# Two FFN projections in seven half-width products instead of eight, for eight of eleven block pairs

## The reference, cut to what matters

```python
def swiglu_ffn(h, w_in, w_out):                 # fa; h = rms_norm(x, g), hidden 2816
    gate, up = jnp.split(h @ w_in, 2, axis=-1)
    return (jax.nn.silu(gate) * up) @ w_out

def swiglu(h, w_gate, w_up, w_down):            # fb and fc, same sizes
    return (jax.nn.silu(h @ w_gate) * (h @ w_up)) @ w_down
```

## Time and profile before

| | |
|---|---|
| median of 3 runs | 2423.3 us (2422.54 to 2423.92) |
| span of the profiled execution | 2420.5 us |
| time around that span, by the median | 2.8 us |
| TensorE busy | 2397.5 us |
| VectorE, ScalarE, GpSimd busy | 1263.9, 1002.5, 331.9 us |
| bytes read | 231.83 MB |

### The profile page before, as it was taken

One profiled execution on the slowest core, in us unless ns is written; L12 is line 12 of the kernel. 1 busy time (PEld: TensorE's weight loads), 2 busy tenths in 40 slices (PEclk: granted clock), 3 DMA queues, 4 the chain that ended last, 5 costly groups with the idle time before them and its releaser, 6 DMA issues.

```text
span 2420.5 us, 30412 instructions
## 1 busy us (share of the span) xinstructions
PE 2397.5 (99%) x12064; PEld 1956.4 (81%) x12064; DVE 1263.9 (52%) x1907; ACT 1002.5 (41%) x1634; POOL 331.9 (14%) x258
## 2 busy tenths in 40 slices
PE   8999999999999999999999999999999999999998
PEld 7777778777898888888888888888887888888887
DVE  5688746468765455443333544333678555333422
ACT  7766654234563344333223433222644454323321
POOL 0000000555100100111102111101032201101100
PEclk9999999999999999999999999999999999999999
DMA  6221235323665232332323332332322232333231
GB/s 203 71 70 51 86 99 183 113 68 108 200 210 209 96 105 70 105 95 88 96 97 101 99 97 90 96 100 88 111 63 63 87 113 74 101 96 105 97 100 56
DMA packets 172638, 251.65 MB, mean 104 GB/s; under 512 B 11472, under 2 KB 90576, under 8 KB 172496
## 3 DMA queue, kind: packets, MB, share of 16 engines
q1 hardware_dynamic: 171344, 248.13, 32.5%
q10 hardware_dynamic: 1152, 1.57, 0.2%
HBM read 231.83 MB, written 16.78 MB: 103 GB/s over the span
## 4 chain that ended last, share of the span: by engine, by line
PE 96%; DVE 2%; ACT 1%; issue 0%; POOL 0%; DMA 0%; DVEq 0%; SPq 0%; POOLq 0%
PE bank L1170 94%; PE bank L1299 1%; DVE wlo L2030 0%; PE bank L1322 0%; DVE T L2038 0%; PE bank L1447 0%; PE bank L1423 0%; DVE macc L2030 0%; PE bank L1265 0%; DMA raw<-in_w_in 0%; DVE xg L2034 0%; ACT whi L1541 0%; DVE ml L2038 0%; DVE bank L2336 0%; DVE W L2030 0%
## 5 line engine op out<-in xcount | busy, mean ns | idle before, releaser
L1170 PE MATMUL bank<-xh,whi 128*128 128x512 f32 x1784 | 710.1, 398 | 8.0 <-DVE wlo L2030 8.0
L1170 PE MATMUL bank<-xh,wlo 128*128 128x512 f32 x1784 | 696.6, 390 | 0.0
L1170 PE MATMUL bank<-xl,whi 128*128 128x512 f32 x1784 | 695.9, 390 | 0.0
L2030 DVE TENSOR_TENSOR wlo<-raw,whi 128x1024 fp32r<-128x1024 f32 (+2 forms) x406 | 500.2, 1234 | 337.2 <-ACT whi L1541 337.0
L1541 ACT ACTIVATE whi<-raw 128x1024 fp32r<-128x1024 f32 (+2 forms) x406 | 419.2, 1038 | 513.7 <-PE bank L1170 507.2
L1170 PEld LDWEIGHTS bank<-xh,whi 128*128 128x128 f32 x1784 | 335.7, 188 | 94.7 <-issue 20.2
L1170 PEld LDWEIGHTS bank<-xh,wlo 128*128 128x128 f32 x1784 | 335.4, 188 | 71.1
L1170 PEld LDWEIGHTS bank<-xl,whi 128*128 128x128 f32 x1784 | 336.0, 188 | 65.4
L2030 DVE TENSOR_TENSOR T<-bank,R 128x512 f32<-128x512 f32 x86 | 59.0, 687 | 344.3 <-PE bank L1170 344.3
L1170 PE MATMUL bank<-hh,whi 128*128 128x512 f32 (+1 forms) x536 | 206.9, 386 | 0.0
L1170 PE MATMUL bank<-hl,whi 128*128 128x512 f32 (+1 forms) x536 | 206.8, 386 | 0.0
(11 more groups left out here) (356 smaller groups left out, 3494.9 us busy)
## 6 DMA issues: line engine op xcount, KB each, us to landing
raw<-in_w_in SPq DMA_DIRECT2D x92, 512.0 KB, 3.6
raw<-in_w_ffn_in SPq DMA_DIRECT2D x88, 256.0 KB, 3.2
raw<-in_ffn_gate SPq DMA_DIRECT2D x88, 256.0 KB, 2.8
raw<-in_ffn_up SPq DMA_DIRECT2D x88, 256.0 KB, 3.1
raw<-in_ffn_down SPq DMA_DIRECT2D x44, 512.0 KB, 3.6
raw<-in_w_ffn_out SPq DMA_DIRECT2D x22, 512.0 KB, 3.6
raw<-in_w_xattn_kv SPq DMA_DIRECT2D x16, 512.0 KB, 4.4
raw<-in_w_kv_mem SPq DMA_DIRECT2D x16, 512.0 KB, 4.9
```

The source lines that it names most:

```text
L1170: return e.matmul(out, l, r, start=start, stop=stop, skip_group_check=skip)
L2030: return e.tensor_tensor(out, a, b, op)
```

## The change

For blocks 3 to 10 of each FFN the pair of projections is computed in seven products instead of eight (a Winograd form of the 2 x 2 block product). Tokens are cut in halves of 256, the eight row chunks in even and odd ones, the 256 gate and 256 up columns of a block in two tiles of 128 each. Then a product is (four chunks) x (128 gate and 128 up columns) x (256 tokens): 2 x 4 x 3 = 24 matmuls with 256 moving columns, all in one bank, gate in its left half and up in its right one.

- **Operands.** `operands(tag)` makes, beside blocks 0 to 2, the normalized x in quarters, three sums and differences and the high and low parts of all seven, in `xop` (four buffers of 14 x 256): `x_gain`, `op_hi` on ScalarE, `x_norm`, `x_sum`, `op_lo` on VectorE. As R is in them, these blocks need no multiplication by R.
- **Weights.** A block's weights come as two quarters of 1 MB (`load_quarter`; even and odd chunks) to four buffers. Four of the seven weight operands are sums: two on GpSimd (products 5 and 6), two on VectorE (7 and 3). All seven are split as slots are (`s_hi`, `s_lo`), three products ahead.
- **Joins.** ScalarE copies bank a to bank b after product 1 (`seed_b`) and bank b to bank f after product 7 (`seed_f`), and TensorE adds later products onto the copies; it copies two partial results to T buffers (`keep`), which VectorE adds (`c22`, `c12`). Then silu of 256 columns on ScalarE and a multiplication with the up half on VectorE (`s_mul`), four times a block, write `hid`.
- **Banks.** Odd blocks use side, even ones main, and block 1 and d0 are moved to side.
- **Hidden tensor.** `ffn_up` writes `hid`; its high and low parts (`h_hi`, `h_lo`) are made at the end of the seven-product stretch and during d0, as are fb's `x_scaled` steps.
- **Memory.** The DMA scratch is cut to 1 KB so that the buffers fit.

```diff
+        def product_order():
+            order = [(PLAIN, p) for p in (1, 5, 6, 2)]
+            for i in range(PLAIN + 1, 11):
+                order += [(i - 1, 7), (i, 1), (i - 1, 4), (i, 5)]
+                order += [(i - 1, 3), (i, 6), (i, 2)]
+            return order + [(10, 7), (10, 3), (10, 4)]
...
+        def seven(tag):
+            first = SEVEN[tag] + len(PRODUCTS)
...
+            for n, (i, p) in enumerate(PRODUCTS):
...
+                step("product", tag, n)
+                pay()
+                owed.append(lambda i=i, p=p: seven_finished(tag, i, p))
+                point()
+                prepare_sum(tag, n + 4)
+                prepare_last(tag, n + 6)
+                prepare_hi(tag, n + 3)
...
+            def product(tag, n):
...
+                w.wait_ge(*at("w lo", c))
+                if p in (1, 5):
+                    ring, name = seven_ring(i)
+                    w.wait_ge(*free(ring, name, u))
+                elif p in (2, 6):
+                    w.wait_ge(*at("seed b", tag, i))
+                elif p == 7:
+                    w.wait_ge(*at("kept", tag, i, 6))
+                elif p == 4:
+                    w.wait_ge(*at("seed f", tag, i))
+                else:
+                    w.wait_ge(*at("kept", tag, i, 5))
+                for gu in range(2):
+                    out = b[:, 256 * gu:256 * gu + 256]
+                    for k in range(4):
...
+                        a, d = h[:, gu, k, :], l[:, gu, k, :]
+                        t, tl = xopr[k][:, hi, :], xopr[k][:, lo, :]
+                        mm(out, a, t, p in (1, 5) and gu == 0 and k == 0, False, skip=True)
+                        mm(out, a, tl, False, False, skip=True)
+                        ins = mm(out, d, t, False, k == 3, skip=True)
...
+            def seed_b(tag, i):
+                ring, name = seven_ring(i)
+                u, b = seven_bank("b", tag, i)
+                w.wait_ge(*free(ring, name, u))
+                w.wait_ge(*at("product", tag, i, 1))
+                copy(b[:], seven_bank("a", tag, i)[1][:]).then_inc(*up("x_exp", ("seed b", tag, i)))
...
+            def w_sum(tag, i, p):
+                if p not in COMBINED:
+                    return
...
+                if p == 5:
+                    ins = tt(out, part_of(tag, i, 7), part_of(tag, i, 4), ALU.add)
+                else:
+                    w.wait_ge(*at("w sum", tag, i, 5))
+                    ins = tt(out, part_of(tag, i, 5), part_of(tag, i, 1), ALU.subtract)
+                ins.then_inc(*up("ffn_gate", ("w sum", tag, i, p)))
...
         def ffn(tag, out):
...
-            for i in range(11):
+            for i in range(PLAIN):
...
-                        soon(1, "h_lo", tag, 2 * i + m - 2)
-                gemm(f"{tag}{i}", evict)
-            step("mark", f"{tag}d")
+                gemm(f"{tag}{i}", evict, hook=begin_seven(tag) if i == PLAIN - 1 else None)
+            drain(built[0])
+            seven(tag)
+            for x, j in enumerate(range(4, 22)):
+                soon(max(0, 2 * x - 2), split_h, tag, j)
+            if tag == "fb":
+                for k in range(8):
+                    soon(4 + 4 * k, "x_scaled", k)
             gemm(f"{tag}d0", residual(out, 0))
```

More of the change, by code:

```diff
@@ L13 @@
 S = 512
-BASE = 17408
+SCRATCH = 1024
+BASE = SCRATCH + 1024
 EPS = 1e-6
@@ L334, in split_to @@
         def split_to(j):
-            while ready[0] < min(j, NS):
+            while ready[0] < min(j, upto[0]):
                 load_to(ready[0] + NR)
@@ new lines, in begin_seven, with hook @@
+        def begin_seven(tag):
+            def hook(n):
+                if n == 4:
+                    for i in range(PLAIN, 11):
+                        for e in range(2):
+                            step("quarter", tag, i, e)
+                if n in (11, 13, 15):
+                    prepare_hi(tag, (n - 11) // 2)
+                if n in (12, 14):
+                    prepare_sum(tag, n // 2 - 5)
+            return hook
+        def seven(tag):
+            first = SEVEN[tag] + len(PRODUCTS)
+            ready[0] = loaded[0] = first
+            upto[0] = min([x for x in SEVEN.values() if x > first] + [NS])
+            for n, (i, p) in enumerate(PRODUCTS):
+                ring = seven_ring(i)[0]
+                if p == 1:
+                    for b, letter in enumerate("aebf"):
+                        ring.new(letter, tag, i, among=(b,))
+                    for b, what in enumerate(("even", "odd", "c22", "u2")):
+                        (tmp2 if i % 2 else tmp).new(what, tag, i, among=(b,))
+                step("product", tag, n)
[5 more added lines that the diff above has]
+                prepare_hi(tag, n + 3)
+                if (i, p) == (8, 5):
+                    split_h(tag, 0)
+                if n >= PLACE[9, 3] + 3:
+                    split_h(tag, n - PLACE[9, 3] - 2)
+                if n + 3 >= len(PRODUCTS):
+                    split_to(first + n + 4 - len(PRODUCTS))
+            step("mark", f"{tag}d")
@@ L935, in ffn, with build @@
         def ffn(tag, out):
+            built = []
+            def build():
+                built.append(start(operands(tag), 3))
             if tag == "fb":
@@ L956, in ffn, with ahead @@
             else:
-                later(1, norm(tag))
+                def ahead():
+                    norm(tag)()
+                    soon(5, build)
+                later(1, ahead)
             step("mark", f"{tag}")
-            for i in range(11):
+            for i in range(PLAIN):
                 def evict(m, i=i):
@@ L1887, in ffn_gate, with h_hi @@
                 e.activation(t[:], t[:], ACT.Silu).then_inc(*up("ffn_silu", ("ffn silu", tag, j)))
-            def ffn_up(tag, j):
-                n, t = tmp("gate", tag, j)
+            def h_hi(tag, j):
+                w.wait_ge(*at("h done", tag, j))
+                if 0 < j < 5:
+                    for q in (11, 22, 21, 12):
+                        w.wait_ge(*at("s mul", tag, 9, q))
+                elif j > 4:
+                    w.wait_ge(*at("product", tag, 10, 3))
+                copy(hh[j][:], hid[j][:]).then_inc(*up("h_hi", ("h hi", tag, j)))
@@ new lines, in op_hi, with s_hi @@
+            def op_hi(tag, kp, part):
+                t, tr = xop[kp], xopr[kp]
+                if part == 0:
+                    w.wait_ge(*at("x norm", tag, kp))
+                    ins = copy(tr[:, 11:14, :], t[:, 8:11, :])
+                else:
+                    w.wait_ge(*at("x sum", tag, kp))
+                    w.wait_ge(*at("op lo", tag, kp, 0))
+                    ins = copy(tr[:, 7:11, :], t[:, 0:4, :])
+                ins.then_inc(*up("x_hi", ("op hi", tag, kp, part)))
+            def s_hi(tag, n):
+                i, p = PRODUCTS[n]
+                c = SEVEN[tag] + n
+                if p in (1, 2, 4):
+                    w.wait_ge(*at("quarter", tag, i, 0 if p == 1 else 1))
+                else:
+                    w.wait_ge(*at("w sum", tag, i, p))
+                w.wait_ge(*at("w used", c - NH))
+                copy(eight(shi[c % NH][:]), part_of(tag, i, p)).then_inc(*up("w_hi", ("w hi", c)))
```

316 lines of the change are left out of this document (286 added, 30 removed).

## The result

The changed kernel takes 2393.6 us (median of 4 runs, 2392.6 to 2396.5) where the kernel before takes 2422.9 on the same chip: ratio 0.9881, 95% interval 0.9867 to 0.9895, or 29.3 us less. The forecast was 2389.5 and 33.7 us. The profiled execution has a span of 2390.8 us, 29.7 under the one before.

The account below looks back on a forecast made before the run. TensorE, busy 99% of the span, was taken as the bound. 38.2 us saved in blocks less 4.5 at entries gives 33.7 off 2420.5, 2386.8; with 2.8 carried over, 2389.6, rounded 2389.5 us; range 2382 to 2408.

Parts of the forecast that it names:

- the largest term of the sum: TensorE in the changed blocks: 1.59 us saved a block, 38.2 us for 8 blocks x 3 FFNs.
- The rate: TensorE block by block: a plain block takes 21.67 us, a changed one 20.08 at 0.1195 us a matmul.
- Rival 3: TensorE in changed blocks: a matmul is paid by its columns alone, 60 us saved, 2363 us; chance 0.03.
- The other engines: Per changed block: ScalarE 11.4 us, VectorE 14.4 and up to 18.5 with contention, all hidden within TensorE's 20.1.
- The joins: TensorE's new waits for copies or joins at five of seven products: 0 us in steady state, 2 us spare.
- Rival 1: The joins leak in changed blocks: one wait late by 0.6 to 1.2 us, 14 to 29 us in all; chance 0.17.
- The weights: Quarter loads in the changed blocks: 4 to 7 us each, 0 us cost, but the steady chain's least cover.
- The entry: Start of each FFN's eight changed blocks: late second weight sum and bank copy, 4.5 us for three FFNs, bounds 0 and 9.
- 1.5 with what follows: Loss at each FFN's entry: 1.4 us taken for the late sum and copy, 1.5 including what comes after.
- the contention: GpSimd and VectorE slow one another in changed blocks: VectorE loses at most about 4 us a block, hidden.
- Exit: Hidden tensor's high and low parts moved to the down projection: TensorE needs nothing of it early, 0 us.

Follow-up runs that it names:

- the narrow kernel: Changed kernel with 192 of 256 moving columns in every matmul of the seven-product stretch; one run, 0.1117 us between starts, no whole time given.
- Five plain blocks: Changed kernel with five plain blocks instead of three in each FFN, six changed blocks fewer in all: 2401.36 us, 9.4 us slower than the changed kernel.
- the seven doubled low parts: Changed kernel with each low part of a weight operand computed twice on VectorE, in all seven products: 2514.75 us, 123 us slower than the changed kernel.
- a second copy: Changed kernel with each of a block's four bank copies made twice on ScalarE: 2393.53 us, 1.6 us slower than the changed kernel.
- The early second sum: Changed kernel with product 6's first-block sum issued ahead of the last two gate multiplications on GpSimd: 2388.48 us, 3.5 us faster than the changed kernel.
- the sums on VectorE: Changed kernel with all four weight sums of a block on VectorE, none on GpSimd: 2385.89 us, 6.1 us faster than the changed kernel.
- keeping the third one back: Sums on VectorE plus early second sum, with the second block's first quarter not loaded until the first block's quarters are there: 2385.64 us.
- the kernel with four copies: Changed kernel with each of a block's four bank copies made four times on ScalarE: 2411.93 us, 20 us slower than the changed kernel.

## Why the prediction was right, and where it was off

The mechanism was right: TensorE's rate sets the blocks, the other engines are hidden, and the loss is at the entries. That the largest term of the sum came out to 0.2 us was luck, two misreadings that cancel.

**The rate.** A changed block was put at 168 x 0.1195 = 20.08 us and takes 20.16, at 0.1200 a start: in the two stretches of the earlier trace rows the first few steps are shorter, and the others are 0.120. A plain block was put at 96 x 0.2257 = 21.67 and takes 21.76, by the count that was read too high. Each term is too low by 0.08 or 0.09 us, and so their difference, the saving, is 1.60 us where 1.59 was predicted: 38.4 in all against 38.2. Had only one of them been read rightly, the sum would have been off by some 2 us. Rival 3, columns alone, is out twice over, by the rate and by the narrow kernel. With it goes the Trainium skill's 262 cycles for 256 columns (TensorE: Matmul & The Clock Gate, Back-to-back issue gap) as a price for this stream: 109 ns there, which the page calls the gap of an isolated matmul, and 120 here. Five plain blocks show the saving per block by a timing of its own.

**The other engines.** ScalarE was put at 11.4 us a block and has 10.8; VectorE at 14.4 plus at most 4 and has 15.6; GpSimd at up to 5.8 when alone and has 5.6. Nothing of it is on the path, and the seven doubled low parts show where it would be.

**The joins.** "0 us in steady state, 2 us spare" is right: no wait in 21 of 24 blocks, a second copy free, and three more cost a steady block 0.09 us. Rival 1 didn't happen.

**The weights.** 0 us in the steady part, right. The cover was thinner at fb's entry than said, below.

**The entry.** This is the term that was mis-sized: 4.5 us predicted, 2.3 + 3.3 + 2.3 = 7.9 measured. The first wait comes at the place and in the size worked out. GpSimd and VectorE at fa's entry in the changed kernel, first product at 1037.35 (T):

```profile
1035.45 1.30 POOL L3141 TENSOR_TENSOR T<-T,R 128x512 f32<-128x512 f32 x1 [2.43 <-ACT T L2097]
1036.92 2.07 POOL L3141 TENSOR_TENSOR T<-T,R 128x512 f32<-128x512 f32 x1 [0.17 <-ACT T L2097]
1038.95 2.39 POOL L3141 TENSOR_TENSOR wsum<-wsum,quarter 128x1024 f32<-128x1024 f32 x1
1042.98 2.95 POOL L3141 TENSOR_TENSOR wsum<-quarter,quarter 128x1024 f32<-128x1024 f32 x1 [1.64 <-DMA quarter<-in_w_ffn_in]
```

```profile
1042.46 1.22 DVE L2314 TENSOR_TENSOR slo<-wsum,shi 128x1024 fp32r<-128x1024 f32 x1 [2.75 <-ACT shi L1751]
1043.61 3.41 DVE L2314 TENSOR_TENSOR quarter<-quarter 128x1024 f32<-128x1024 f32 x1
1046.94 2.42 DVE L2314 TENSOR_TENSOR slo<-quarter,shi 128x1024 fp32r<-128x1024 f32 x2
```

The second sum stands behind both gate multiplications and ends at T+4.0 (T+3.1 to T+4.2 predicted), its low part at T+6.3 (T+5.6 to T+6.7). ScalarE's first bank copy, behind two high parts, ends at T+6.5 (T+6.0 to T+7.1) and is what TensorE waits for last, until T+6.7. That is the wait of 1.0. Two errors partly cancel in it: the gate multiplications end at T+1.6, not T+0.3, and the sum takes 2.4 us where 2.8 to 3.9 were allowed. The second wait, 1.4 us, wasn't foreseen; "1.5 with what follows" left 0.1 for it. VectorE's own sum for product 7 takes 3.41 us instead of 1.22: GpSimd has begun the next block's sum at 1042.98. The VectorE instruction ends 1.1 us after GpSimd's does (1045.93 to 1047.02), as if it had begun only then. The early second sum and the sums on VectorE both remove it, by different ways. The prediction had the contention as a loss in the mean, up to 4 us a block, and not as one instruction's delay where nothing is spare; the mean was right (15.6 us of work within 18.5) and the moment was missed. The third miss was fb. The chain that ended last, at fb's entry in the changed kernel (start us, us, what), shows it:

```profile
1374.28 1.23 DVE xopr L2314
1375.51 1.15 DVE wlo L2314
...
1378.25 6.42 DMA quarter<-in_ffn_up
...
1384.79 2.41 POOL wsum L3141
```

The quarters' transfer waits for the last plain block's last low part (1375.51) and takes 6.4 us, and the sum for product 5 starts 4 us before the first product, where fa's started 7 us before it (1030.16). VectorE's operand work stands in front of that low part, but it isn't what sets fb apart: the low part ends 12.1 us before the first product, and fa's 12.8. The buffers do. The first quarter leaves at

```profile
1376.73 0.37 SPq L3350 DMA_DIRECT2D quarter<-in_ffn_gate  x1
```

which is 12.0 us before the first product; in fa and fc it leaves 23.7 before it. A first quarter takes the place of two of the last plain block's four slots, and an FFN has 12 + 56 + 22 = 90 slots, two more than a multiple of the four buffers. So in fa and fc these are the block's first two slots, and in fb its last two. That is why three quarters leave together in fb and share the transfer, and keeping the third one back removed the last wait. The prediction's four to seven us for a quarter, and its cover, were for the steady part; at fb's entry it had no term for this.

**Sum.** 33.7 predicted, 0.2 more for the blocks, 3.4 less for the entries: 30.5, which is what the stretches show. Outside them 0.8 are lost: 29.7.

**Exit.** 0 us, right: the rate of the down projection is unchanged.

## What to carry to other kernels

A product that is halved to save columns pays its fixed part twice: take the distance between starts of the shorter form from a trace before counting the saving, for here an eighth fewer columns brought 7% of the block's time. Where a chain of products has slack of several products in steady state, look for the loss at its entry, where the last work of the old kind and the first of the new stand in the same queues. Work moved to GpSimd isn't free for VectorE, even while GpSimd is idle over 70% of the time: here the engine that was to be relieved had less to do without the help. And a rate is read from two starts and the number of steps between them, not from a window's count: here two matmuls too many in 443 hid a tenth of a microsecond in every block.

## What the runs showed that I had not expected

- A VectorE instruction with two inputs in SBUF that begins during a GpSimd sum ends only after it: 3.41 for 1.22 us, and 2.62 us for a multiplication of 256 elements that otherwise takes 0.42. All 18 of these multiplications that begin during a sum in the changed kernel take 2.62 or 2.63. Timeline of the changed kernel, GpSimd, then VectorE:

```profile
1069.17 3.17 POOL L3141 TENSOR_TENSOR wsum<-wsum,quarter 128x1024 f32<-128x1024 f32 x1 [2.45 <-DVE quarter L2314]
```

```profile
1070.00 2.62 DVE L2314 TENSOR_TENSOR hid<-T,T 128x256 f32<-128x256 f32 x1
```

  It ends 0.28 us after the sum; instructions of 1024 elements end 1.1 us after it, so most of their own work comes behind it. With a bank as one input, `hid<-bank,T` stays at 417 ns. The Trainium skill says as much (SBUF — State Buffer, Who interferes with whom): two SBUF inputs contend, and the order of issue decides who blocks. The trace agrees on the order too: 21 low parts of weight operands during which a sum begins keep their 1.22 us.
- From 256 to 192 columns a matmul with its own weight load gains 0.008 us of 0.120, and one with a single column takes 0.112 as well. Below 256 columns there is next to nothing to win in this form.
- Behind a wait of 3.3 us the granted clock was 0.50 in one entry and 1.00 in others with a wait as long, and a wait of 2.1 us in the kernel with four copies had 0.50 behind it. I have no rule for which it will be.
